# Five places for raw weights and lower parts, four for upper parts, in a decoder trunk on one core

## The reference

```
per layer (2 layers, alpha = 4 ** 0.25):
  x = LN(alpha*x + 0.5 * (silu(x @ w_gate) * (x @ w_up)) @ w_down)     # ffn1
  x = LN(alpha*x + Mix(x))    # layer 0: block-sparse attention and retention; layer 1: S5 scan and GLU
  x = LN(alpha*x + 0.5 * (silu(x @ w_gate) * (x @ w_up)) @ w_down)     # ffn2
LN(x) = (x - mean) * rsqrt(var + 1e-5) * g + b
```

## Time and profile before

| what | value |
|---|---|
| median of 3 runs | 2470.32 us (2470.2 to 2471.86) |
| the profiled execution | 2471.69 us |
| its span | 2470.0 us |
| TensorE matmul busy | 2366.2 us (96%), 18943 instructions |
| TensorE weight load busy | 2252.9 us (91%) |
| VectorE busy | 1622.1 us (66%) |
| ScalarE busy | 1081.8 us (44%) |
| GpSimd busy | 465.0 us (19%) |
| mean granted clock of TensorE | 0.986 |
| DMA | 417.85 MB, mean 169 GB/s |

### The profile page before, as it was taken

The page is one execution under the profiler, slowest core; times in us unless marked ns, Lnnn a source line. Parts: engine busy times, 40 slices in busy tenths (PEclk is TensorE's granted clock), DMA queues, the critical chain, the costliest instruction groups (busy, mean ns, idle before and its releaser), DMA issues.

```text
span 2470.0 us, 46567 instructions
## 1 busy us (share of the span) xinstructions
PE 2366.2 (96%) x18943; PEld 2252.9 (91%) x18943; DVE 1622.1 (66%) x2539; ACT 1081.8 (44%) x1633; POOL 465.0 (19%) x535
## 2 busy tenths in 40 slices
PE   7989999999899999999999999999999999999998
PEld 6988998999789777888999999999999998999997
DVE  4796776666675656678677476477556594487555
ACT  3433344433554433452454534554333537354332
POOL 4896720000300022200202001031002010221001
PEclk9999999999999999999999999999999999999998
DMA  8667776445345798544565555555554566554553
GB/s 176 174 173 205 196 194 193 136 116 146 111 148 177 239 308 259 147 131 121 170 180 163 171 161 184 177 166 145 155 153 138 189 184 212 156 164 145 152 147 106
DMA packets 676422, 417.85 MB, mean 169 GB/s; under 512 B 31570, under 2 KB 639698, under 8 KB 676210
## 3 DMA queue, kind: packets, MB, share of 16 engines
q1 hardware_dynamic: 669682, 394.51, 55.3%
q0 software_dynamic: 6528, 20.37, 2.7%
HBM read 396.04 MB, written 18.78 MB: 168 GB/s over the span
## 4 chain that ended last, share of the span: by engine, by line
PE 76%; DVE 13%; ACT 4%; issue 3%; DMA 2%; SPq 1%; POOL 1%; DVEq 0%; ACTq 0%; POOLq 0%
PE ps L270 21%; PE ps L272 20%; PE ps L271 20%; DVE w_lo L265 4%; PE ps L1004 2%; PE ps L1006 2%; PE ps L1005 2%; ACT w_hi L256 2%; PE ps L2410 1%; DMA w_raw<-in_ffn_w_up 1%; DVE h_lo L467 1%; DVE x L557 1%; PE ps L1742 1%; PE ps L1165 1%; PE ps L2393 1%
## 5 line engine op out<-in xcount | busy, mean ns | idle before, releaser
L265 DVE TENSOR_TENSOR w_lo<-w_raw,w_hi 128x1024 fp32r<-128x1024 f32 (+1 forms) x648 | 826.8, 1280 | 612.1 <-ACT w_hi L256 608.9
L270 PE MATMUL ps<-x_hi,w_hi 128*128 128x256 f32 (+1 forms) x3200 | 970.4, 303 | 32.3 <-DVE w_lo L265 18.9
L271 PE MATMUL ps<-x_lo,w_hi 128*128 128x256 f32 (+1 forms) x3200 | 955.3, 299 | 0.0
L272 PE MATMUL ps<-x_hi,w_lo 128*128 128x256 f32 (+1 forms) x3200 | 955.1, 298 | 0.0
L256 ACT ACTIVATE w_hi<-w_raw 128x1024 fp32r<-128x1024 f32 (+1 forms) x648 | 670.3, 1035 | 582.2 <-PE ps L272 419.1
L270 PEld LDWEIGHTS ps<-x_hi,w_hi 128*128 128x128 f32 x3200 | 615.8, 192 | 50.8 <-DVE w_lo L265 35.0
L271 PEld LDWEIGHTS ps<-x_lo,w_hi 128*128 128x128 f32 x3200 | 616.0, 192 | 1.1 <-issue 0.2
L272 PEld LDWEIGHTS ps<-x_hi,w_lo 128*128 128x128 f32 x3200 | 615.6, 192 | 0.0
L270 PE MATMUL ps<-h_hi,w_hi 128*128 128x256 f32 (+1 forms) x1408 | 423.2, 301 | 14.4 <-DVE w_lo L265 10.9
L271 PE MATMUL ps<-h_lo,w_hi 128*128 128x256 f32 (+1 forms) x1408 | 414.6, 294 | 0.0
L272 PE MATMUL ps<-h_hi,w_lo 128*128 128x256 f32 (+1 forms) x1408 | 414.6, 294 | 0.0
(11 more groups left out here) (281 smaller groups left out, 2137.7 us busy)
## 6 DMA issues: line engine op xcount, KB each, us to landing
w_raw<-in_ffn_w_gate SPq DMA_DIRECT2D x176, 512.0 KB, 4.3
w_raw<-in_ffn_w_up SPq DMA_DIRECT2D x176, 512.0 KB, 3.9
w_raw<-in_ffn_w_down SPq DMA_DIRECT2D x128, 512.0 KB, 3.9
w_raw<-in_w_in_ab SPq DMA_DIRECT2D x56, 512.0 KB, 3.8
w_raw<-in_ffn_w_down SPq DMA_DIRECT2D x64, 384.0 KB, 3.3
arena<-in_cache_k SPq DMA_DIRECT2D x64, 256.0 KB, 5.1
arena<-in_cache_v POOLq DMA_DIRECT2D x64, 256.0 KB, 5.0
w_raw<-in_w_out_ab SPq DMA_DIRECT2D x16, 512.0 KB, 3.8
```

Of the source, the lines that this page charges most:

```text
L265: dve.tensor_tensor(T.w_lo[:, u % RING, 0:n], T.w_raw[:, u % RAW, 0:n], T.w_hi[:, u % RING, 0:n].bitcast(F32), ALU.subtract).then_inc(T.w_ ...
L270: pe.matmul(out, w_hi, m_hi, start=first, stop=False)
L271: pe.matmul(out, w_hi, m_lo, start=False, stop=False)
L272: return pe.matmul(out, w_lo, m_hi, start=False, stop=last)
```

## The change

- **Places.** `w_raw` and `w_lo` now have five places each and are the same memory: `w_lo` of a piece is written over its `w_raw`. `w_hi` has four places. The total is as before, nine pieces. The load of piece u waits until TensorE has used piece u - 5.
- **Leads.** ScalarE and VectorE work three pieces ahead (`LEAD = 3`), SyncE issues up to piece u + 4 in the step of piece u (`AHEAD = RINGS - 1`). There is one load semaphore for each of the five places.
- **Order on VectorE.** In a gate and up step the second split stands behind `gate` (L455).
- **Start.** Five pieces are issued before the S5 constants. The norm weights are loaded as 48 rows of 512 bytes on SyncE's queue and transposed on TensorE with the S5 constants; the two loads on GpSimd's queue go. TensorE does 12 matmuls of ones before x is there, and two after each block of transposes. The first roundings and splits stand one block earlier.
- **Taps.** The eight stores of taps of one q are spread over three steps: 2, 3, 3.
- **End.** The sum over the partitions is one matmul of the sum of blocks 0 to 6 and one of block 7; GpSimd's last addition goes. Only blocks 0 to 2 are added up as squares; TensorE reduces that sum and the squares of blocks 3 to 7 one by one, so 18 matmuls in place of 6. TensorE does 2 and 6 matmuls of ones between. The root's table is loaded ahead of the squares. ScalarE scales 2 blocks and VectorE 6 (before: 4 and 4). The second half is transposed and written first.
- **Semaphores.** `h_rounded`, `zeroed` and `rs_zeroed` are replaced by the chain semaphore of VectorE, with the same waits.

```
-RAW, RING = 3, 3
-LEAD = 2
+LOADING, RINGS, RING = 5, 5, 4
+LEAD = 3
...
+    here = (T.nc.sbuf_base + 31) // 32 * 32
+    T.w_lo = sb("w_lo", [P, RINGS, PIECE], F32R)
+    T.w_raw = T.nc.alloc_sbuf_tensor_at("w_raw", [P, RINGS, PIECE], F32, offset=here)
...
-        if u >= RAW:
-            sp.wait_ge(T.w_split.h, u - RAW + 1)
-        sp.dma_start(dst, src).then_inc(T.w_loaded[u % RAW].h, 16)
+        if u >= RINGS:
+            sp.wait_ge(T.w_used.h, u - RINGS + 1)
+        sp.dma_start(dst, src).then_inc(T.w_loaded[u % LOADING].h, 16)
...
-AHEAD = RAW + LEAD
+AHEAD = RINGS - 1
...
+def warm(T, pe, n, bank=NORM_BANK):
+
+    for _ in range(n):
+        pe.matmul(T.ps[:, bank, 0:P], T.ones[:, :], T.ones[:, :], start=True, stop=True)
...
-            rest_piece(T, dve, u + 1 + LEAD)
             gate, prod = T.gate[:, i % 2, 0:g.n], T.prod[:, i % 2, 0:g.n]
             dve.wait_ge(T.tanh_done.h, Q.tanh + i + 1)
             dve.scalar_tensor_tensor(gate, gate, 1.0, T.ps[:, T.banks[o], 0:g.n], ALU.add, ALU.mult)\
                .then_inc(T.silu_done.h, 1)
+            rest_piece(T, dve, u + 1 + LEAD)
...
+        pe.wait_ge(T.acc_added.h, self.added + KT - 2)
+        pe.matmul(self.ps, T.ones[:, :], self.acc, start=True, stop=False)
+        warm(T, pe, 2, 7)
+        pe.wait_ge(T.res_done.h, res + KT)
+        pe.matmul(self.ps, T.ones[:, :], self.x(KT - 1), start=False, stop=True).then_inc(T.sum_done.h, 1)
...
+        warm(T, pe, 6, 7)
+        first = True
+        for k in (SUMMED, SUMMED + 1, SUMMED + 2, None, *range(SUMMED + 3, KT)):
...
+            squares = self.acc2 if k is None else self.sq[:, k, :]
+            for i, t in enumerate(self.g.tiles):
...
+        act.activation(self.by_row[:, 0:1], self.eps, ACT.Sqrt)
...
-            q = self.at(i, 4)
-            if q is not None:
+            for part, taps in enumerate((range(0, 2), range(2, 5), range(5, CL))):
+                q = self.at(i, 4 + part)
+                if q is None:
+                    continue
                 sp.wait_ge(S.placed.h, q + 1)
-                for t in range(CL):
+                for t in taps:
...
+        for r, name in enumerate(("ln_g", "ln_b")):
+            q.dma_start(self.gain_rows[0:NORMS, r, :], I[name].rearrange("l r (k p) -> (l r k) p", p=P))\
+             .then_inc(self.T.ln_loaded.h, 16)
...
-            load_pieces(T, sp, RAW)
+            load_pieces(T, sp, LOADING)
...
-            load_pieces(T, sp, RAW + 8)
+            load_pieces(T, sp, LOADING + 6)
...
+            pe.wait_ge(T.const_ready.h, 1)
+            warm(T, pe, FIRST_WARM)
             pe.wait_ge(T.const_loaded.h, 16)
-            run(load_tensor(T, pe, A, rows, turned[A]))
+            for _ in load_tensor(T, pe, A, rows, turned[A]):
+                warm(T, pe, 2)
```

More of the change, by code:

```diff
@@ L369, in __init__ @@
         self.u, self.o = len(T.pieces), len(T.banks)
-        self.tanh, self.silu, self.glu, self.rounded, self.h = (
-            c.take(n) for c in (T.tanh_done, T.silu_done, T.glu_done, T.h_rounded, T.h_done))
+        self.tanh, self.silu, self.glu, self.h = (
+            c.take(n) for c in (T.tanh_done, T.silu_done, T.glu_done, T.h_done))
         self.res_before = None if part == 0 else F.res
@@ L751, in __init__ @@
         self.places = halves(g)
+        self.order = (3, 4, 5, 0, 1, 2)
     def bank(self, n):
@@ L787, in gpsimd @@
         T = self.T
-        for k in range(1, 4):
+        for k in range(1, SUMMED):
             pool.wait_ge(T.squared.h, self.squared + k + 1)
@@ L799, in scalar @@
             act.activation(self.sq[:, k, :], self.x(k), ACT.Square).then_inc(T.squared.h, 1)
-        for k in range(4):
+        for k in range(SCALED):
             act.activation(self.x(k), self.x(k), ACT.Copy, scale=self.gain(k)).then_inc(T.scaled.h, 1)
@@ L823, in vector @@
         dve.wait_ge(T.const_loaded.h, 2 * 16)
[L824 to L827, removed]
+        for i, n in enumerate(self.order):
+            t, q, m = self.places[n]
+            cols, of = slice(q * 512, (q + 1) * 512), t - self.g.tiles[0]
+            dve.wait_ge(T.y_turned.h, turned + (1 if q else 2))
+            dve.scalar_tensor_tensor(rows[0:m, t, cols], T.ps[0:m, self.bank(n), :], self.by_row[0:m, of:of + 1],
                                      self.bias_rows[0:m, cols], ALU.mult, ALU.add).then_inc(T.y_moved[0].h, 1)
@@ L831, in sync @@
         T = self.T
-        for n, (t, q, m) in enumerate(self.places):
+        for i, n in enumerate(self.order):
+            t, q, m = self.places[n]
             cols = slice(q * 512, (q + 1) * 512)
-            sp.wait_ge(T.y_moved[0].h, moved + n + 1)
+            sp.wait_ge(T.y_moved[0].h, moved + i + 1)
             dst = y_prompt[t * P:(t + 1) * P, :] if t < PT else y_sample
@@ L2067, in sync @@
         S = self.S
-        for i in range(self.STEPS):
+        for i in range(self.STEPS + 2):
             q = self.at(i, 3)
@@ L2157, in vector @@
                 for n in range(2):
[L2158 to L2159 removed]
+                    T.dve_chain(dve, dve.memset(self.kernel[n][0:GH, :, 0:P], 0.0))
             q = self.at(i, 3)
@@ L2648, in tensor @@
         pe.wait_ge(self.spread.h, 1)
+        pe.wait_ge(T.ln_loaded.h, 32)
+        for r in range(2):
+            pe.transpose(T.ps[:, NORM_BANK, 2 * P + r * NORMS:2 * P + (r + 1) * NORMS], self.gain_rows[0:NORMS, r, :],
+                         T.ident[0:NORMS, 0:NORMS])
         for r in range(3):
```

99 lines of the change are left out of this document (47 added, 52 removed).

## The result

The changed kernel is slower: 2485.64 us median (2478.15 to 2494.43, 18 runs) against 2471.97 (2468.80 to 2481.73, 18 runs) on the same chip, ratio 1.0051, 95% interval 1.0041 to 1.0061. The profiled execution has a span of 2481.4 us against 2470.0.

A forecast was written before the change was run, and what follows sets the result against it. TensorE's idle and half-clock time was taken as the bound. Terms 7.2 + 3 + 9 + 21 + 4 - 2 = 42.2 us off 2471.7 gave 2429.5 for the profiled execution and 2428 for the median, range 2408 to 2460.

The forecast's parts named there:

- What bounds it: Whole kernel: TensorE sets the time; its idle time and half-clock stretches, in few places, are what can be won.
- Start, 7.2: First 60 us: without the 4-byte loads piece 1 lands earlier, ones hold full clock; gain 7.2 us, between 3 and 15.
- 110 to 165, 3: From 110 to 165 us, VectorE full: one further piece of lead, spent once, gains 3 us, between 0 and 6.
- the first rival: VectorE's load, not its lead, is the bound; where full, a piece in hand saves once or nothing; 2451, chance 0.25.
- 165 to 270, 9: From 165 to 270 us: earlier loads and spread tap stores remove two of three long waits; 9 us, between 0 and 14.
- After 275, 21: After 275 us: most of 26.1 us of waits for splits go, with two half-clock stretches; 21 us, between 0 and 29.
- the two clusters: After 275 us, 11.3 us of split waits where norm or scan work fills VectorE; one piece each goes, 2.2 and 2.9.
- End, 4: End: sum's matmuls and transposes at full clock, first output tile at about 2459.1 in place of 2463.1; gain 4 us.
- its own lower case, half clock: End: if the matmuls of ones do not hold the clock, the end is worth nothing or costs 1 us.
- What it costs, 2: Where a norm is waited for, three or four places: later loads make `x` 0.4 late; cost 2 us, between 0 and 6.
- Loads start too late: Rival: loads hang on TensorE's use; landing over 8.2 us slows every piece of group A; 2486, chance of slower 0.08.
- It doesn't do what it says: Rival: SyncE still stands, side stores still hold loads, only the end and some single waits gain; 2467, no separate chance given.

The follow-up runs named there:

- stand only: Six and three, with each rounding from piece 72 on also waiting for the load of the piece two further on; 2483.54 us.
- six and three: Changed kernel with six places for loads and lower parts, three for upper parts, rounding two pieces ahead, a further SyncE wait before decay stores; 2453.43 us.
- all but rings: Changed kernel with places, leads and the loads' wait for the split put back as before, all else as changed; 2457.21 us.
- lead two: Changed kernel with rounding and splitting two pieces ahead in place of three, and a further SyncE wait before decay stores; 2458.23 us.
- four and two: Changed kernel with four places for loads and lower parts, four for upper parts, rounding two pieces ahead, a further SyncE wait before decay stores; 2495.86 us.
- more ones: Six and three with two matmuls of ones ahead of each block of squares but the first, ten more in the end; 2450.74 us.
- old taps, no ones: All but rings, with the eight tap stores in one step again and no matmuls of ones at start or end; 2462.52 us.

## Why the prediction was wrong, by its steps

*What bounds it.* Right: TensorE's idle and half-clock time is what can be won or lost. In stand only against six and three the weight load's waits grow by 21.0 us in all and the granted clock takes 9.7 us more (time by one less the clock), together the 30.4 us between their spans.

*Start, 7.2.* The size was right for all but the rings, 7.6 up to tanh 8, and of the mechanism the part of the small loads; the ones, which were to bring the first piece to full clock, added nothing (7.7 without them). Piece 1 is rounded at 11.19, its load no longer behind the 4-byte loads (ScalarE; answers to the earlier trace rows), the S5 wait stays at 2.5, and the wait for a split is at 55.3 in place of 60.2 (53 forecast):
```profile
11.19 1.04 ACT L257 ACTIVATE w_hi<-w_raw 128x1024 fp32r<-128x1024 f32 x1
```
The rings took 4.2 of it back; 3.4 is left. The wait for x_lo shrank to 2.2 us, it did not go.

*110 to 165, 3.* 3.7 from tanh 8 to 15, where lead two has 2.5 more than before. That is not the third piece of lead alone: four and two, with a lead of two, has 0.9 less than before there. The kernels that come early to tanh 8 lose in this stretch, and from the start to tanh 15 the changed kernel has 7.1 us less than before, all but rings and lead two 5.9, six and three 7.4. And it was lent. At 157.8 TensorE waits for `h_lo`, and VectorE has no idle time ahead of it; weight load and VectorE in order of time:
```profile
PEld ps L271 <- DVE h_lo L476: 5.8, 1, 5.8
```
```profile
153.43 1.95 DVE L266 TENSOR_TENSOR w_lo<-w_raw,w_hi 128x1024 fp32r<-128x1024 f32 x1
155.30 0.41 DVE L471 SCALAR_TENSOR_TENSOR prod<-gate,ps 128x256 f32<-128x256 f32 x1
155.75 0.74 DVE L475 CAST h_hi<-prod 128x256 fp32r<-128x256 f32 x1
156.52 1.20 DVE L476 TENSOR_TENSOR h_lo<-prod,h_hi 128x256 fp32r<-128x256 f32 x1
```
Before, the wait for `h_lo` at this point was 2.1 us: 3.7 gained, 3.7 given back. Where VectorE is full, the first rival is right, and lead is worth nothing. It is busy 50.9 of 55 us. The Trainium skill's page "SBUF — State Buffer" (Who interferes with whom) says that a VectorE instruction with two SBUF inputs contends with a GpSimd instruction that reads SBUF. The splits' median of 1980 ns against a shortest of 1214 agrees with it again, and so does the whole trace of the changed kernel: of its 648 splits the 478 beside which GpSimd ran nothing took 1.23 us at most, and 95 of the other 170 took longer:
```profile
L266 DVE TENSOR_TENSOR w_lo<-w_raw,w_hi x16: 1214/1980/2314, 109.8 to 160.2; 128x1024 fp32r<-128x1024 f32 x16
```

*165 to 270, 9.* 0.4 (tanh 15 to 24, with the 3.7 given back in it, so 4.1); 6.9 without the rings. The stores are spread as meant, the load between them is issued in time and the clock is 1.00 (SyncE; answers to the earlier trace rows):
```profile
192.65 1.95 SPq L2117 DMA_DIRECT2D s_made_taps<-arena  x3
194.65 0.59 SPq L242 DMA_DIRECT2D w_raw<-in_ffn_w_gate  x1
195.28 0.62 SPq L242 DMA_DIRECT2D w_raw<-in_ffn_w_up  x1
```

*After 275, 21.* From tanh 24 to 191 it is 19.9 us the other way. Splits came earlier, 14.2 us of their waits went (18 or more were forecast). Of the two clusters one went from 5.5 to 4.3 us; in the other the 5.8 us of waits for splits went, but TensorE's waits of all kinds there are 10.1 in place of 8.4 us. So splits in time were of no use by themselves: what was lost stood in other waits, and in the clock.

*End, 4.* 1.0. The chain that ended last (start, us; answers to the earlier trace rows):
```profile
2462.38 0.54 PE ps L783 x2
...
2463.36 0.56 PE ps L786 x2
...
2466.18 4.98 PE ps L799 x36
2471.16 5.33 PE ps L809 x24
...
2476.51 0.75 DVE arena L855
```
The squares' matmuls begin 4.1 us after the last ffn matmul (4.4 forecast), but the 36 take 4.98 us, not 3.6: 0.14 each, and the clock is down before they end. So the transposes are at half clock, 2.97 us to the first tile as before, and that tile is at 12.0, not at 9 (13.4 before). From the first tile to the end it is 0.4 us longer than before, in which the new order of the tiles may have a part. The term was mis-sized; its own lower case, half clock, was the nearer.

*What it costs, 2.* This is the step that failed, and with it the 21 of *After 275*. It asked when the last consumer, TensorE, would miss the piece: "the load of piece u+3 lands 1.0 us after TensorE starts piece u", and priced the delay of one instruction, `x`. It did not ask the question for the first consumer: that 1.0 us is ScalarE standing at every step, with tanh, the copies and exponentials of the attention, and then VectorE's queue behind it. It stood for 602.8 us in all, 328 times. The runs put the rings, less what they gain, at a loss of 28 us with the other parts in place and of 53 without; putting back the standing alone costs 30.

*Rivals.* "Loads start too late" (0.08) named the right part and landed at 2486, but by a formula for TensorE, with 8.2 us of landing as the point from which it decides. Landing stayed at a median of 3.8 in the quiet stretch and 4.7 from 165 to 270. The point is the distance of one piece, 2.9 us in group A, which every load exceeds. "It doesn't do what it says" is out: the loads are issued when the edit says.

The prediction named its own refutation, "if ScalarE's waits for loads turn into TensorE's". They did, as waits for keys; the longer wait for `h_lo` at 157.8 stands behind a full VectorE.

## What to carry to other kernels

A prefetch has a distance to each consumer, and the one that counts is that to the first engine that waits for it in order. More lead in a later stage with the same number of places is taken from the loads: before a stage is moved ahead, compare issue to turn with issue to landing, and list what is queued behind the wait. When places are fixed, give them to the raw data (six, and three for the results) rather than to lead. Parts of a change can mask each other: the order of two instructions was worth 17, 6 or 0 us in kernels where ScalarE stood for loads 570, 110 and 3 us.

## What the runs showed of the hardware

The granted clock fell while TensorE had no gap. In the kernel with more ones it is 1.00 up to 2437, 0.88 in the next 2 us and 0.50 after that, over a stream of matmuls of 1 and of 128 columns without idle time. TensorE's last gap, 0.94 us, had ended at 2435.26, 3.2 us before the fall. The Trainium skill's page "TensorE: Matmul & The Clock Gate" (What's actually happening) ties the clock to how busy the engine has been; by that one would expect this stream to hold it, and the measurement goes the other way, so a busy TensorE in the profile is not enough to call its clock safe. Whether the gap or the kind of matmul brought the fall isn't shown. Without any ones, the clock is down already while the first of the squares' matmuls run (old taps, no ones):
```profile
2436.00:2439.00 3.00, 1.07 (x3) 0.30 (x2) 2.10 (x6) 1.32 (x4) 0.38 (x1) 1.00 0.00 0
2439.00:2442.00 3.00, 2.51 (x13) 2.48 (x13) 3.00 (x10) 2.84 (x7) 1.35 (x2) 0.53 0.00 0
```
Counted from the last tanh the clock falls at 28.1 us there, and at 32.2 in all but rings, which differs in the ones and the tap stores. Among the seven other kernels with the same new end it falls at 29.9 to 32.2; with more ones, at 31.7. So the ones put the fall off by 2 to 4 us and don't prevent it, and ten more don't move it.

A matmul of one column takes 0.13 us at full clock and 0.20 at half; TensorE in the changed kernel, its first 18:
```profile
2466.18 2.29 PE L799 MATMUL ps<-ones,arena 128*128 128x1 f32 x18 [0.94 <-ACT arena L831]
```
So the clock is worth less than a factor of two on such instructions, which the prediction had taken at 0.10.
